# A two-layer decoder trunk with product-key experts: the embedding's stages laid over more ticks of the expert stream, the mixer's over fewer

## What is computed

```python
mix = mixer_block(x, ...)                       # 10 heads: GLA, retention, HGRN2; W_in, recurrences, W_out
x = layer_norm(ALPHA * x + mix, ln1_g[i], ln1_b[i])
x = layer_norm(ALPHA * x + peer_ffn(x, ...), ln2_g[i], ln2_b[i])
x = x + jnp.einsum('blp,pd->bld', p[i], ple_proj[i]) * jax.nn.sigmoid(
    jnp.einsum('bld,de->ble', x, ple_gate[i]))  # the per-layer input embedding

def peer_ffn(x, w_q, subkeys, u_tab, v_tab):    # per token 8 heads x 16 experts of 16384
    q = x @ w_q; s1, s2 = scores of the two halves of q against 128 subkeys each
    v1, i1 = top_k(s1, 16); v2, i2 = top_k(s2, 16)
    best, ci = top_k(v1[:, None] + v2[None, :], 16)
    expert = i1[ci // 16] * 128 + i2[ci % 16]
    act = gelu(einsum('thkd,td->thk', u_tab[expert], x))
    return einsum('thk,thkd->td', softmax(best) * act, v_tab[expert])
```

## Time and profile before

| | us |
|---|---|
| median of 3 runs | 3875.31 |
| lowest, highest | 3865.82, 3877.32 |
| the profiled execution, its own time | 3870.57 |
| its span in the trace | 3868.8 |
| PE busy, DVE busy, POOL busy, ACT busy | 3249.1, 2751.3, 2462.5, 960.8 |

### The profile page before, as it was taken

One profiled execution on the slowest core, in us unless ns is written; L12 is line 12 of the kernel. 1 busy time (PEld: TensorE's weight loads), 2 busy tenths in 40 slices (PEclk: granted clock), 3 DMA queues, 4 the chain that ended last, 5 costly groups with the idle time before them and its releaser, 6 DMA issues. The chain is left out here.

```text
span 3868.8 us, 40078 instructions
## 1 busy us (share of the span) xinstructions
PE 3249.1 (84%) x12692; PEld 1894.8 (49%) x12692; DVE 2751.3 (71%) x6289; ACT 960.8 (25%) x1960; POOL 2462.5 (64%) x2164
## 2 busy tenths in 40 slices
PE   8797597988987689788898589999899769786887
PEld 7576363555554366344465256555556324322433
DVE  1636889886478988778568996788657878845443
ACT  2421131332122223223222122233311223212211
POOL 0102556777776656867776655777877677777773
PEclk9888798998998899998899789999899899999999
DMA  5025898999999899989999989999999999999996
GB/s 182 33 87 198 286 365 317 344 344 368 365 371 396 288 339 375 353 314 323 350 373 411 326 287 346 348 355 334 379 353 366 381 340 367 407 374 352 376 403 250
DMA packets 331042, 1269.90 MB, mean 328 GB/s; under 512 B 38336, under 2 KB 39616, under 8 KB 313808
## 3 DMA queue, kind: packets, MB, share of 16 engines
q0 software_dynamic: 299520, 1090.65, 75.7%
q1 hardware_dynamic: 31312, 176.67, 11.8%
HBM read 1259.74 MB, written 7.44 MB: 328 GB/s over the span
## 5 line engine op out<-in xcount | busy, mean ns | idle before, releaser
L849 PE MATMUL Y<-GV,DIAG 128*128 128x512 f32 x3308 | 1704.5, 653 | 402.7 <-DMA GV<-in_vtab,IDX 348.7
L1035 POOL DMA_INDIRECT GU<-in_utab,IDX x1024 | 1179.1, 1151 | 563.2 <-issue 272.9
L1035 POOL DMA_INDIRECT GV<-in_vtab,IDX x1024 | 1179.6, 1152 | 550.2 <-issue 240.2
L1787 DVE SCALAR_TENSOR_TENSOR GU<-GU,X 128x1024 f32<-128x1024 f32 x1024 | 1237.6, 1224 | 356.4 <-DMA GU<-in_utab,IDX 354.1
L849 PEld LDWEIGHTS Y<-GV,DIAG 128*128 128x128 f32 x3308 | 645.0, 206 | 1231.8 <-issue 1000.8
L544 PE MATMUL A<-XT,WR 128*128 128x264 f32 (+1 forms) x2496 | 580.7, 390 | 22.5 <-ACT R L1257 10.8
L544 PEld LDWEIGHTS A<-XT,WR 128*128 128x128 f32 x2496 | 483.2, 194 | 144.7 <-issue 73.8
L1291 ACT ACTIVATE DIAG<-C,WGT 128x128 f32<-128x128 f32 x827 | 299.5, 391 | 548.9 <-PE Y L849 359.9
L1832 DVE SCALAR_TENSOR_TENSOR YS<-GV,WGT,YS 128x1024 f32<-128x1024 f32 x197 | 256.2, 1301 | 49.0 <-DMA GV<-in_vtab,IDX 31.1
L763 PE MATMUL D<-WR,R 96*128 96x256 f32 (+3 forms) x800 | 191.3, 397 | 14.6 <-POOL R L1009 14.6
L763 PEld LDWEIGHTS D<-WR,R 96*128 96x128 f32 (+3 forms) x800 | 143.4, 181 | 71.6 <-issue 18.3
(11 more groups left out here) (214 smaller groups left out, 2885.8 us busy)
## 6 DMA issues: line engine op xcount, KB each, us to landing
WR<-in_wstream SPq DMA_DIRECT2D x96, 1024.0 KB, 8.0
WR<-in_wstream SPq DMA_DIRECT2D x36, 1280.0 KB, 9.5
GU<-in_utab,IDX POOLq DMA_INDIRECT x1024, 6.6
GV<-in_vtab,IDX POOLq DMA_INDIRECT x1024, 6.7
R<-in_lnp SPq DMA_DIRECT2D x14, 512.0 KB, 8.6
SS<-in_st_in SPq DMA_DIRECT2D x12, 384.0 KB, 6.5
out_st_s<-SS SPq DMA_DIRECT2D x12, 384.0 KB, 6.8
WR<-in_wstream SPq DMA_DIRECT2D x16, 256.0 KB, 6.8
```

The source lines that it names most:

```text
L849: last = nc.tensor.matmul(Y[0:rows, c], scaled, GV[:, v % RV, c], start=(j == 0), stop=(j == end - 1))
L1035: pool.indirect_dma_start(ring[:, i % places, :], None, table, bass.IndirectOffsetOnAxis(ap=idx, axis=0)).then_inc(fetched[i % places], 16)
L1787: nc.vector.scalar_tensor_tensor(out=u, in0=u, scalar=1.0, in1=X[:, tile_of(g), :], op0=ALU.mult, op1=ALU.mult, accum_out=SCORE[:, g % 2, ...
```

## The change

The weights of the embedding's stages are 1.5 times as large (4.0 of the small ones to 6.0, 4.4 to 6.6, and 3.0 to 4.0 for the sample tile's pg). No instruction is added or taken away.

```diff
 def embedding_stages(e):
     tiles = EMBED[e][3]
-    out = [(("ln2", e, n), 4.0) for n in tiles]
-    out += [(("n2", e, n), 4.0) for n in tiles]
-    out += [(("x2t", e, n), 4.0) for n in tiles]
-    out += [(("pg", e, c, n), 4.4 if n < 4 else 3.0) for c in range(4) for n in tiles]
+    out = [(("ln2", e, n), 6.0) for n in tiles]
+    out += [(("n2", e, n), 6.0) for n in tiles]
+    out += [(("x2t", e, n), 6.0) for n in tiles]
+    out += [(("pg", e, c, n), 6.6 if n < 4 else 4.0) for c in range(4) for n in tiles]
     return out
```

## The result

The changed kernel takes 3908.92 us (median of 7 runs, 3898.3 to 3917.35) against 3875.31 for the kernel before (7 runs, 3853.87 to 3886.53). The ratio is 1.0091, with a 95% interval of 1.0073 to 1.0110: slower by about 35 us, in the range and on the side that was forecast, and more than the forecast's +21. The profiled execution has a span of 3896.5 us, 27.7 more than before.

What follows compares the result with a forecast made beforehand. DVE was taken as the bound while the embedding runs beside the searches, PE right behind. Step 1's +6 and step 2's +15 made +21 us on 3870.6, 3891.6, set at 3894; own range 3880 to 3914, with rivals 3862 to 3918.

Steps and rivals of the forecast that it cites:

- DVE sets the pace in the embedding's stretches: Ticks 24 to 56 of step 1 and 24 to 64 of step 2: DVE is the bound, -3 us each.
- PE work enters the stretches behind: Step 1, ticks 56 to 80 +5 us and 80 to 104 +4; step 2, ticks 64 to 104 +12.
- Behind tick 104 of step 2: 8.2 us of PE work come in there, partly hidden: +6 us, ends 0 and +9.
- PE takes over at about tick 41: Step 2 of the kernel before: PE sets the pace from about tick 41 to about tick 91.
- Step 1 would keep its loss: Step 1 loses 6 us in all, and nothing changes behind its tick 104.
- The wait that would go away: Rival: DVE's waits before L1423, 33 us over both steps, come off the time, giving 3859; chance 0.14.
- the gaps of DVE take the loss up: Rival: PE slack and DVE's gaps in the embedding leave only +6 us, 3877 to 3879; chance 0.2.
- The clock in the embedding's stretches: Rival: thinner PE work lowers the granted clock; at 0.6 it adds +6 and +15 us, 3914; chance 0.08.

Runs made afterwards that it cites:

- late_mixer: Kernel before with an empty stage after embeddings kept at nearly their old ticks, so the mixer starts as late as in the changed kernel; ratio 1.0087.
- wide_step2: Kernel before with the larger weights in the embedding of step 2 only, the sample tile's pg at 4.5; ratio 1.0052.
- half_gate_before: Kernel before with half of the gate's matmuls (4 of 8 of each pg) left out in the embeddings of steps 1 and 2; ratio 1.0001.
- wide_step1: Kernel before with the larger weights in the embedding of step 1 only; ratio 1.0038.
- later_decay: Kernel before with the DVE stage that begins with L1423 moved 3 and 4 ticks later in mixers 2 and 3; ratio 1.0011.
- dense_step1: Kernel before with weights 0.67 times as large in the embedding of step 1 alone; ratio 0.9952.
- wide_twice: Kernel before with the weights of both embeddings 2 times as large; ratio 1.0143.
- half_gate_after: Changed kernel with half of the gate's matmuls left out in the embeddings of steps 1 and 2; ratio 1.0081 against the kernel before.

## Why the prediction was right, and where its sizes were off

The mechanism was the forecast's: PE work left stretches paced by DVE and entered stretches in which it is the bound. The sizes were too small in nearly every term. The stretches make +37 us for +21, just beyond the sum of all outer ends (-3 + 10 + 7 - 3 + 16.4 + 9 = +36.4). By these ends the forecast's own range is 3880 to 3909, not to 3914, and the time of 3908.92 us is at its very end; it lies well inside only by the wider range that the rivals gave.

**DVE sets the pace in the embedding's stretches: right.** Lengths of 124.6 and 152.5 us stood against 124 and 157. The terms were -3 and -3, the trace has -2.0 and -7.0.

**PE work enters the stretches behind: right in sign, too small.** Ticks 56 to 80 +8.0 us for +5 (ends 3 and 10), ticks 80 to 104 +5.9 for +4 (ends 0 and 7), ticks 64 to 104 of step 2 +19.3 for +12 (ends 10.5 and 16.4). In that last term PE's work grew by 18.0 us for the 16.4 reckoned, and PE's idle time did not close: 7.3 us for 5.9. The term that was mis-sized is this one, by the choice of the lower end, with the reason that 109.9 us passed without a gap already. In ticks 56 to 80 of step 1, too, PE was not full as foretold: 94.0 of 98.9 us, with its 4.9 idle us all in ticks 56 to 60, ahead of the late z stages.

**Behind tick 104 of step 2: half the size.** +12.8 us for +6 (ends 0 and 9); against the 506.5 to 510.4 us of kernels that don't differ there it is +9 to +13. I had let the idle 31.8 us hide part of the 8.2 us that come in, and none was hidden: late_mixer and wide_step2 show +12.6 and +9.8, too. In ticks 104 to 184, which took 264.5 us before and 274.3 now, PE's work grew by 9.6 us and its idle time stayed (15.8 and 16.0). In the rest of the step PE had 3.8 us less work by the records, and its idle time grew from 16.0 to 22.9. That the mixer's further stages are 3% closer may be in these numbers, and no run separates it.

**"PE takes over at about tick 41": wrong.** The time of 2287 us is tick 43, but the tick is the smaller error. half_gate_before took 14 us of PE work out of ticks 24 to 64 of step 2 and changed nothing. DVE makes the pace nearly up to the first z stages. The forecast did not suffer, since its terms for that stretch were taken from DVE alone.

**Step 1 would keep its loss: right, against the single trace.** +11.9 us in the trace up to tick 104, +15 us in the times of wide_step1.

**The rivals.** The wait that would go away grew in step 1, and later_decay showed that moving it brings nothing; but the place had its meaning: the wait is what the z chain has left over, 12.8 us before, 18.8 now and 0 in dense_step1. That the gaps of DVE take the loss up has fallen with the result itself, and in wide_twice the embedding's stretches hardly gained more.

The clock in the embedding's stretches stayed at 0.88 and 0.89, so that this rival never came to be where it was looked for; half_gate_after had 86.6 and 109.2 us of PE there, at 0.86 and 0.85, and the same lengths. It had a second place that the prediction did not name, the stretch behind: ticks 56 to 80 of step 1 ran at 0.95 now for 1.00 before, ticks 80 to 104 at 0.87 for 0.93. But over the z stages themselves, which set the time there, the clock is 0.97 now for 0.96 before in step 1, and 0.98 for 1.00 in step 2 (the rows below). So it can have made them 1.6 us longer in step 2 (69.6 for 68.0) and no longer in step 1 (68.4 for 73.0). What it costs behind the z stages no run separates. The rule of the Trainium skill, "TensorE: Matmul & The Clock Gate", Part 1, asks to keep PE's work dense. It points to the right side here, since a denser embedding raised the clock to 0.94 and one of twice the width had 0.85 and 0.83; but the thinner one of the change did not lower it, and late_mixer shows the loss without it.

**What remains as the mechanism.** The z stages are some 70 us of PE work with their rows of the stream (from 1402.6 to 1475.6 us before, 1433.0 to 1501.4 now, by the first and last start of L544), and PE has no gap in them. DVE must not pass L1423 before they are done. Up to tick 68 DVE has the searches to do, its ticks are long, and PE's chain fits behind them; a chain that starts later comes out from under long DVE ticks and stands beside short ones. The start of L544, first and last, before and after:

```profile
L544 PE MATMUL A<-XT,WR x208: 378/380/765, 1402.6 to 1475.6; 128*128 128x256 f32 x104
```

```profile
L544 PE MATMUL A<-XT,WR x208: 379/379/764, 1433.0 to 1501.4; 128*128 128x256 f32 x104
```

Relative to tick 24 the chain ends 19.6 us later, (1501.4 - 1301.5) for (1475.6 - 1295.3). How much DVE does beside the z stages tells the rest. These are the z stages of step 1 and of step 2, first before, then changed, and last step 1 of dense_step1:

```profile
1402.60:1475.60 73.00, 73.00 (x268) 52.83 (x269) 59.71 (x174) 11.56 (x31) 40.97 (x39) 0.96 0.91 343
2341.10:2409.10 68.00, 67.99 (x259) 49.22 (x260) 43.41 (x109) 11.25 (x29) 41.44 (x37) 1.00 0.98 369
...
1433.00:1501.40 68.40, 68.39 (x260) 50.39 (x261) 44.81 (x123) 12.68 (x31) 39.86 (x35) 0.97 0.92 334
2382.20:2451.80 69.60, 69.60 (x259) 50.19 (x260) 26.08 (x43) 11.16 (x28) 39.86 (x36) 0.98 0.94 353
...
1378.00:1449.70 71.70, 71.70 (x271) 51.35 (x272) 65.51 (x194) 13.67 (x35) 45.23 (x41) 1.00 0.99 371
```

DVE's work beside the z stages fell by 14.9 us in step 1 and by 17.3 in step 2, where ticks 56 to 104 and 64 to 104 took 13.9 and 19.3 us more; in late_mixer it is 44.9 and 24.2 us, as in the changed kernel, and in dense_step1 it rose by 5.8. The overlap of the two engines that is lost is of the size of the loss. That is read from the traces; the experiment behind it is late_mixer, which moves the projections and leaves the embedding nearly where it was.

## What to carry to other kernels

When two engines take turns as the bound, ask of a move in which of the two regimes the moved engine's work lies now and where it comes to lie: here the later start of the projections cost in both steps, and the same edit in the other direction gained in the step where PE still had room in the embedding's stretch, and lost in the one where it had none. A PE that the records show busy without a gap, and a chain of waits that runs over it, do not make it the bound; leaving half of a stage's matmuls out tells it in one run, if the clock is read beside it. Change such a table one place at a time: the gain of one step (-19 us) had been hidden by the loss of the other.

## What the runs showed of the hardware

PE's granted clock is not the same from execution to execution of the same instructions. Ticks 104 to 208 of step 1 took from 344.2 to 363.3 us in the traces of kernels that don't differ there, at mean clocks from 0.93 down to 0.86, with PE busy for 288.8 to 311.4 us. The clock is a part of this scatter and not all of it: 344.2 us had the highest clock, but 363.3 us stood at 0.88 and 361.9 at 0.86. Where DVE paced, or PE was full, the same instructions took 159.5 to 160.8 us (five traces) and 142.2 to 143.4 (three). So a single trace's span can hide a third of an effect of this size, and the stretches it concerns, beside timed runs, show it.
